# Six half tiles of the output projection between the steps of the last pair of heads, where there were four

## What is computed

```python
def forgetting_attention(xn, w_q, w_o, k, v, c):
    ...
    for blk in range(S // Q_BLOCK):
        ...
        s = s + c[:, :, q0:q1, None] - c[:, :, None, :q1]
        s = jnp.where(mask, s, -jnp.inf)
        p = jax.nn.softmax(s, axis=-1)
        outs.append(jnp.einsum('bhqk,bhkd->bhqd', p.astype(v.dtype), v[:, :, :q1]))
    o = jnp.concatenate(outs, axis=2).transpose(0, 2, 1, 3).reshape(B, S, D_MODEL)
    return o @ w_o
...
        h = h + mix
        h = h + swiglu(rmsnorm(h, norm_ffn[layer]), w_ffn_in[layer], w_ffn_out[layer])
```

## Time and profile before

| | us |
|---|---|
| median of 3 runs | 2283.23 |
| lowest, highest | 2282.92, 2284.03 |
| the profiled execution | 2281.58 |
| its span, first to last instruction | 2279.8 |

### The profile page before, as it was taken

How to read it: one execution, slowest core, us unless ns; L and a number is a source line. 1 busy time by engine, 2 the same in 40 slices (tenths; PEclk the granted TensorE clock), 3 DMA queues, 4 the chain that set the end, 5 groups by cost and what they waited for, 6 DMA issues and landing times.

```text
span 2279.8 us, 31817 instructions
## 1 busy us (share of the span) xinstructions
PE 2230.7 (98%) x10537; PEld 1840.1 (81%) x10537; DVE 1674.2 (73%) x2217; ACT 1182.1 (52%) x1871; POOL 363.4 (16%) x355
## 2 busy tenths in 40 slices
PE   8999999999999999999999999989999999999998
PEld 7888877888878888878888888877888888788886
DVE  7667788788777777687666666664767888788865
ACT  5543466355545555265656665653535555455534
POOL 4000000022222222021111111102102222222200
PEclk9999999999999999999999999999999999999999
DMA  5121201366666666331111101122135666566652
GB/s 149 47 65 36 75 19 38 129 130 128 129 115 130 130 130 130 111 121 29 29 38 37 37 28 37 28 93 65 56 125 101 130 128 129 119 128 127 130 163 84
DMA packets 208854, 208.13 MB, mean 91 GB/s; under 512 B 9688, under 2 KB 153280, under 8 KB 208704
## 3 DMA queue, kind: packets, MB, share of 16 engines
q0 software_dynamic: 39168, 75.51, 20.1%
q1 hardware_dynamic: 167808, 126.43, 18.6%
q10 hardware_dynamic: 1728, 4.31, 0.7%
HBM read 122.28 MB, written 83.95 MB: 90 GB/s over the span
## 4 chain that ended last, share of the span: by engine, by line
PE 88%; DVE 7%; ACT 2%; issue 2%; DMA 1%; ACTq 0%; POOL 0%; DVEq 0%
PE ps L1208 36%; PE ps L1040 15%; PE ps L1296 13%; PE ps L1409 11%; PE ps L1456 3%; PE ps L1443 3%; PE ps L1543 2%; PE ps L1424 2%; PE ps L1421 1%; DVE rxl L2228 1%; DVE resid L2248 1%; PE ps L1382 1%; PE ps L1522 0%; DVE sq_ffn L2682 0%; DVE xl L2232 0%
## 5 line engine op out<-in xcount | busy, mean ns | idle before, releaser
L973 POOL DMA_DIRECT2D spill<-c x256 | 223.6, 925 | 739.1 <-DVE c L2618 509.6
L2487 DVE TENSOR_TENSOR ring_l<-raw_ffn,ring_h 128x512 fp32r<-128x512 f32 x320 | 222.6, 697 | 155.8 <-ACT ring_h L1770 155.4
L1770 ACT ACTIVATE ring_h<-raw_ffn 128x512 fp32r<-128x512 f32 x320 | 199.1, 626 | 192.4 <-PE ps L1208 99.6
L1863 ACT ACTIVATE c<-ps 128x512 f32<-128x512 f32 x256 | 149.3, 598 | 14.4
L3028 DVE TENSOR_TENSOR ptl<-ps,pth 128x512 fp32r<-128x512 f32 (+1 forms) x160 | 97.3, 635 | 72.3 <-ACT pth L2144 71.5
L1409 PE MATMUL ps<-xh,wh_att 128*128 128x512 f32 x368 | 149.6, 406 | 0.0
L2109 ACT ACTIVATE probs<-ps,nmax 128x896 f32<-128x896 f32 (+7 forms) x128 | 94.8, 741 | 103.4 <-DVE nmax L3022 102.8
L1770 ACT ACTIVATE ring_h<-w_sum 128x512 fp32r<-128x512 f32 x112 | 69.6, 625 | 149.2 <-DVE w_sum L2513 39.9
L1409 PE MATMUL ps<-xh,wl_att 128*128 128x512 f32 x368 | 144.4, 392 | 0.0
L1409 PE MATMUL ps<-xl,wh_att 128*128 128x512 f32 x368 | 144.1, 392 | 0.0
L2618 DVE TENSOR_TENSOR c<-ps,c 128x512 f32<-128x512 f32 x192 | 123.6, 686 | 4.7 <-PE ps L1296 4.4
(11 more groups left out here) (404 smaller groups left out, 6389.3 us busy)
## 6 DMA issues: line engine op xcount, KB each, us to landing
spill<-c POOLq DMA_DIRECT2D x256, 256.0 KB, 5.9
raw_ffn<-in_w_ffn_in SPq DMA_DIRECT2D x88, 512.0 KB, 5.3
raw_ffn<-in_w_ffn_out SPq DMA_DIRECT2D x44, 512.0 KB, 7.5
resid<-spill SPq DMA_DIRECT2D x24, 512.0 KB, 7.7
raw<-in_w_rec_in SPq DMA_DIRECT2D x16, 512.0 KB, 5.6
spill<-resid POOLq DMA_DIRECT2D x16, 512.0 KB, 2.9
raw_att<-in_w_kvf SPq DMA_DIRECT2D x16, 512.0 KB, 4.0
xin<-in_x SPq DMA_DIRECT2D x4, 1024.0 KB, 9.7
```

What stands on the lines that cost most here:

```text
L973: pool.dma_start(spill[m, :, half * BANK:(half + 1) * BANK], block[:, :], accum_op=ALU.add).then_inc(sem, 16)
L1770: act.activation(F.ring_h[slot][:, :], src, ACT.Copy).then_inc(F.unit_hi, 1)
L1863: act.activation(dst[:, :], y if what == "s5" else w, ACT.Copy).then_inc(out_tapped, 1)
L2487: dve.tensor_tensor(F.ring_l[slot][:, :], src, F.ring_h[slot][:, :].bitcast(F32), ALU.subtract).then_inc(F.unit_lo, 1)
```

## The change

Two more half tiles, (2, 0) and (2, 1), are summed between the steps, so the last pair has 42 p and not 28: 14 more letters p in the table of units, two in each of the units 0 and 2 to 6, one in unit 1 and one in unit 7. The work in front of pair 7's terms is then tile 3's sum over pairs 0 to 6 and not tile 2's; tile 3 goes with 6 products behind it as tiles 0 to 2 do, and four full tiles remain.

Tile 2's weights take slot 8 (`raw_f`, `wh_f`, `wl_f`), tile 3's slot 5 as tile 2's did. Tile 1's weights are split on DVE in unit 1 behind T0 and not in unit 2 behind O; tile 2's on ACT in unit 3, on DVE in unit 4. Behind the pair the first weights to be split are tile 4's, after tile 1 and not after tile 0. The PSUM slots are 1, 2, 1, 0, 2, 1, 0, 2: tile 2 now takes the slot of tile 0.

```diff
 LAST_UNIT_STEPS = [
-    "T0 T1 X Y p p p T2 V0 V1 T3 S0 S1 p V2 p V3",
-    "O T0 S0 S1 p V0 p",
-    "O T0 T1 S0 p V0 T2 S1 p V1 p V2 p",
-    "O T0 T1 S0 S1 p V0 p V1 p",
-    "O T0 T1 p p V0 T2 p V1 T3 S0 p V2 S1 p V3",
-    "O T0 S0 S1 p V0 p",
-    "O T0 T1 S0 p V0 T2 S1 p V1 p V2 p",
-    "O T0 T1 R p V0 p V1 p",
+    "T0 T1 X Y p p p T2 p V0 V1 T3 S0 S1 p p V2 p V3",
+    "O T0 S0 S1 p p V0 p",
+    "O T0 T1 S0 p p V0 T2 S1 p V1 p p V2 p",
+    "O T0 T1 S0 S1 p p V0 p V1 p p",
+    "O T0 T1 p p V0 T2 p V1 T3 S0 p p V2 S1 p p V3",
+    "O T0 S0 S1 p p V0 p p",
+    "O T0 T1 S0 p p V0 T2 S1 p V1 p p V2 p",
+    "O T0 T1 R p p V0 p V1 p",
 ]
-EARLY_PARTS = [(0, 0), (1, 0), (0, 1), (1, 1)]
+EARLY_PARTS = [(0, 0), (1, 0), (0, 1), (1, 1), (2, 0), (2, 1)]
...
-    pieces.plan("attZ", [7]).plan("attE", [6, 7, 5, 6, 7, 6, 7, 6])
+    pieces.plan("attZ", [7]).plan("attE", [6, 7, 8, 5, 7, 6, 7, 6])
...
-    .plan("attE", [1, 2, 0, 1, 2, 0, 1, 2, 2])
+    .plan("attE", [1, 2, 1, 0, 2, 1, 0, 2, 2])
...
-    OUT_HI_AT = {(-1, "A"): 0, (0, "S1"): 1, (UNITS - 1, "T0"): 2}
-    OUT_LO_AT = {(-1, "S1"): 0, (2, "O"): 1, (UNITS - 1, "T1"): 2}
+    OUT_HI_AT = {(-1, "A"): 0, (0, "S1"): 1, (3, "S1"): 2, (UNITS - 1, "T0"): 3}
+    OUT_LO_AT = {(-1, "S1"): 0, (1, "T0"): 1, (4, "T0"): 2, (UNITS - 1, "T1"): 3}
+    NEXT_OUT = {1: 4, 2: 5, 4: 6, 5: 7}
...
-            for m in range(2):
+            for m in range(3):
                 load(pieces.use("attE", m), att_piece("O", m))
...
-            for m in range(2, 5):
+            for m in range(3, 6):
                 load(pieces.use("attE", m), att_piece("O", m))
...
-                    wo_part(claim(tiles.use("attE", 2)), pieces.use("attE", 2), 0, PAIRS - 1)
+                    wo_part(claim(tiles.use("attE", 3)), pieces.use("attE", 3), 0, PAIRS - 1)
                 if m == 2:
                     pe.wait_ge(f_drained, f_before(PAIRS - 1) + 2 + len(EARLY_PARTS))
+                if m == 3:
                     wo_part(ps[tile[0]], piece, PAIRS - 1, PAIRS).then_inc(out_filled, 1)
-                elif m < 2:
+                elif m < 3:
...
-                if k < KT - 2:
-                    if k != 2:
-                        split_hi(pieces.use("attE", k + (3 if k < 2 else 2)), (out_filled, OUT_ATT + k + 1))
-                else:
+                if k in NEXT_OUT:
+                    split_hi(pieces.use("attE", NEXT_OUT[k]), (out_filled, OUT_ATT + k + 1))
+                elif k >= KT - 2:
```

13 lines of the change are left out of this document (6 added, 7 removed).

## The result

The changed kernel takes 2287.69 us (median of 19 runs, 2285.51 to 2291.92), the kernel before, on the same chip, 2281.05 us (median of 19 runs, 2278.07 to 2286.08). The ratio is 1.0030, with a 95% interval of 1.0024 to 1.0036: the change makes the kernel slower by some 6.6 us (5.5 to 8.2), which is more than the 0.2% that can be told from no change. The predicted time, 2287.4, is only 0.3 us from the measured one, but part of that is luck. The kernel before ran 2.2 us faster here than in the three runs that the forecast started from, and the step that I gave, +4.2 us, is 2.4 us short of the measured one.

The account below looks back on a forecast made before the run. PE, busy for 98% of the span, was taken to bound the kernel. The terms +9.65 (pair), -7.5 (behind it) and +2.0 (clock) made +4.2 us, on 2283.23 giving 2287.4 us, range 2282.2 to 2290.8.

Parts of the forecast that it names:

- the moved work: Into the last pair: 14 more p cost 9.8 us; behind it 42 products fewer save 9.5 us.
- The signs: Wrong if pair ends under 8 us later, L3057's first row needs no DMA, or projection's end moves under growth less 6.
- Step 1: Units 0 and 1: the first addition waits for the residual's reload and delays the row maxima; +3.9 us.
- Step 2: Unit 2: half tile (0, 1)'s first p waits about 2.4 us for DVE to empty `f_ps`; delay now +4.9 us.
- Step 3: Unit 3: half tile (0, 1)'s last p waits 0.7 us for `low_o` 7; delay now +5.7 us.
- Step 4: Units 4 to 7: six more p, two holes filled, a 0.65 us wait in unit 6; delay now +9.65 us.
- Step 5: Behind the pair: four full tiles follow, not five, the first after 2.9 us idle; -7.5 us.
- Step 6: PE's clock falls behind the first and third long waits, costing 0.5 and 1.5 us; +2.0 us.
- the rival of three falls: The clock falls behind all three long waits, also the one in unit 2: +5.7 us, 2288.9 us, chance 0.22.
- no clock falls: Rival: the clock stays high behind all the long waits: +2.2 us, 2285.4 us, chance 0.20.
- the load isn't last: Rival: in unit 0 the residual lands before DVE needs it: -0.5 us in all, 2282.7 us, chance 0.10.
- the interleaving pays: Rival: the p fill all 7.0 us of holes in the pair, nothing new waits: -4.7 us, 2278.5 us, chance 0.06.

Follow-up runs that it names:

- e1_no_load_wait: The changed kernel with the first half tile's sum sent to a scratch tile, so its addition doesn't wait for the residual's reload: 2283.07 us.
- e7_fill_waits: The changed kernel with 14 and 8 products that nobody reads in PE's waits of 3.75 and 1.88 us, nothing reordered: 2285.59 us.
- e2_tail_slots: The changed kernel with other weight buffers and banks for the tiles behind the pair, tile 4's weights split behind tile 0 again: 2285.99 us.
- e8_fill_tail: The changed kernel with 11 products that nobody reads in front of the first full tile, where PE waited 2.62 us: 2290.97 us.
- e9_two_waits: The changed kernel with the last pair's steps reordered, e2_tail_slots' buffers, tile 1's high weights split in unit 1, other banks for tiles 5 and 6: 2272.58 us.

## Why the prediction was right, and where it was not

- **What bounds the kernel, the moved work:** right. 14 p and the 42 products are the same work in another place, and PE was last nearly everywhere.
- **The signs:** none of the three that would have shown it wrong came. The pair ends 12.0 us later, L3057's first row waits for a DMA, and the end of the projection moves by 6.2 us.
- **Step 1, +3.9 us:** right in its mechanism and its size. The addition starts 1498.65 less the 2.48 us by which the zero lies later, 1496.17, where the forecast had 1496.1; the maxima 1498.71 (1498.7); PE's wait is 3.75 us (3.7). e1_no_load_wait shows that the reload is its cause. What the forecast didn't have is that the reload's time varies: DVE's wait for it was 3.23 us in the changed kernel and 4.35 in e7_fill_waits.
- **Step 2, +4.9 us:** the order of what DVE has in front of the addition is as told. The product comes at 1511.10 on the clock of the kernel before; the forecast had 1510.15, with 0.5 us more for the first fall. The wait is 1.88 us (1.7).
- **Step 3, +5.7 us, with the first fall 6.2:** the p that stood at 1515.12 starts at 1525.62, which is 1523.14 on the clock of the kernel before: +8.0 us, 1.8 more than told. 0.45 us of it were there at the end of step 2. The rest came behind the second wait: from its product to this p it is 12.04 us, in e7_fill_waits, without the fall, 10.79, and the forecast had 10.65. All of the pair's error is in by here.
- **Step 4, +9.65 us, with the fall 10.15:** measured +11.98 at tile 0's terms, so 1.8 us too little, the same as at the end of step 3. What this step itself adds is right, with a wait between (2, 0) and (2, 1) of 0.60 us (0.65).
- **Step 5, -7.5 us, with the fall -6.0:** measured -5.8. The first full tile starts 8.68 us behind tile 0's terms, where the working had 8.66. e2_tail_slots, where it is gone, shows that the buffers, the banks and the place of the splits make this wait.
- **Step 6, +2.0 us: here the forecast failed.** It said that the clock falls behind the first and the third wait, and that the second, with 1.7 us, keeps it. It fell behind all three. The missing term is a fall of 1.2 us by e7_fill_waits. The first cost 0.6 to 0.9 us and not 0.5. For the last 1.5 us were put down; e8_fill_tail has 1.75. What actually happened is the rival of three falls, which had +5.7 us and 0.22; the stretch has +6.2. The reason that I gave for the second wait was its length, 1.7 us. It was 1.88 us long, and behind waits of just that length the clock fell in four profiles and not in a fifth. So the length told less than I took it to; whether 1.7 us would have kept the clock no run shows, only that 1.67 us did once.
- **The other rivals.** That no clock falls is out. That the load isn't last is out as the course of the changed kernel; its price is confirmed in part: the forecast gave it 4.7 us less, and e1_no_load_wait, where the addition doesn't wait, has 3.65 us less in the stretch and 4.5 less by the medians. That the interleaving pays is out for this order. It is right for another one: the holes of 7.0 us can be filled, as e9_two_waits shows, when the additions and splits don't stand in front of the maxima.
- **The level.** The forecast added its step to a median of three runs, 2283.23. The four medians since, of 15 to 26 runs each, lie from 2280.69 to 2281.05. That error of 2.2 us and the missing 2.4 us of the step are of opposite sign: that the two nearly cancel is luck.

## What to carry to other kernels

Products that are put into the holes of an interleaved stretch don't cost their own time alone. Follow each one to the operation that empties its bank, and look at what that operation waits for and what is queued behind it on its engine: here a reload that could be asked for only when DVE's last operation in front of the addition was done held up the row maxima of the next unit. Count what new waits do to the clock as a cost of its own, 0.6 to 1.8 us each here, and give it a chance even for waits that were seen to pass without one. If a move costs more than it should, move the splits and additions before giving up the idea: the same six half tiles made the kernel 6.6 us slower in one order and, with other buffers in the tail, 8.5 us faster in another.
